# Modulation products of a two-block transformer moved from TensorE to GpSimd

## The chip, the cores and the metric

The kernel runs on one core of a Trainium2 chip. The time is that of the device for one execution, in microseconds (us). Three runs of the kernel before gave 2389.13, 2389.92 and 2393.08 us.

## The reference

Two depth layers (`i` = 0, 1) work on x (256 tokens of 1024 features), each with three sublayers: a SwiGLU feed-forward, an attention (forgetting attention in layer 0, dilated attention in layer 1), and a second SwiGLU. A second block without modulation follows. The part that is changed computes, for each layer, a vector of 9216 numbers from the single row c:

```
c_act = jax.nn.silu(c)
mod = (c_act @ mod_w[i] + mod_b[i]).reshape(B, 3, 3, D)
shift, scale, gate = mod[:, :, 0], mod[:, :, 1], mod[:, :, 2]
h = rms_norm(x, norm_g[i, s]) * (1 + scale[:, s]) + shift[:, s]
x = x + MACARON_WEIGHT * gate[:, s] * swiglu(h, ...)      # s = 0, 2; attention with gate alone for s = 1
```

All is float32. mod_w holds 2 x 1024 x 9216 numbers, 75 MB.

## The kernel before, in words

All weights pass through one stream of 411 pieces of mostly 1 MB (4 blocks of 128 rows by 512 columns), in the order in which TensorE (PE) uses them. SyncE issues their DMAs in that order into six buffers (`raw`, RAW = 6): the piece k goes where the piece k-6 lay, and its DMA waits until that one is free, with every later DMA behind it (L1251 to L1255). A weight piece ("w") is split by ScalarE (ACT) into `whi` and by VectorE (DVE) into the remainder `wlo` (three buffers of each, CONV = 3), which frees its raw buffer; PE then does three products of each block with the split activations. A modulation piece ("m") isn't split.

A modulation unit (i, u) is 512 of the 9216 columns, two m pieces (h = 0 and 1, with 4 blocks each). There are 36 units; the first four of layer 0 come before the first norm, the other 32 lie among the work of the sublayers. `mod_unit` lets PE do eight products in float32, the column of silu(c) (32 wide, one column filled) against 512 columns (L1352 to L1360), into four strips of one PSUM bank. ACT copies the bank to `mrow` (L1507), and after the next feature or token step PE turns `mrow` by four transposes (`mod_turn`, L1361), and DVE sums the four strips and adds the bias (L1682). The m piece's buffer is free when PE has done its products.

`stage_order` places the units. The norm of a sublayer has one, between the statistics and the rows (`between` in `norm`), but for the first norm. The first SwiGLU of layer 0 (stage A) has units 4 to 10 after gateup steps 0, 2, 4, 6, 9 and down steps 0 and 2. The forgetting attention (stage B) has unit 11 at its norm, then unit 12 after its first `fox_in` and `fox_f`, 13 and 14 after the second `fox_in`, 15 after the third. The other SwiGLUs with units (stages C, D and F) have one at the norm, one after gateup 0, and, but for F, four more after gateup 3, 6 and 9 and down 1. The dilated attention (stage E) has one at the norm and five behind groups of three projections. A gateup or token projection is two w pieces, a down step one. The shift and scale units must be done before the norm that reads them, the gate units before the sublayer's last update.

At the start of a sublayer is a `barrier`: ACT, DVE and GpSimd (POOL) wait for the last work planned so far on the others. POOL's program otherwise holds only small loads, the rope angles and, in the second block, the bias and decay tables.

Of the kernel before, what the change touches and what calls it, by code (L numbers as in the profile page):

```python
# [13 lines left out]
P = 128  # L14
# [6 lines left out]
CONV = 3  # L21
PIECE = 2048
BIG = 1e30
ALPHA = 4.0 ** 0.25
# [4 lines left out]
    "c_in", "mod_in", "ident_in", "x_in", "small_in", "late_in", "out_st",  # L29
    "const_set", "c_silu", "w_hi", "w_lo", "piece", "mod_mm", "mod_row", "mod_turned", "mod_col",  # L30
    "square", "stat", "diag", "sqrt", "recip", "rows", "scaled", "x_hi", "x_mod", "x_lo", "resid",
# [10 lines left out]
class Plan:  # L42
# [3 lines left out]
    def __init__(self, a):  # L46
        self.a = a
        self.steps = []
        self.count = {}
        self.recent = {}  # L50
        self.pieces = []
        self.next_dma = self.next_conv = self.use = self.n_conv = 0
        self.raw_free = [None] * RAW
        self.conv_free = [None] * CONV
        self.land = [0] * RAW
        self.free = [None] * 8
        self.pair = 0
        self.beside = []
        self.turns = []
        self.mod_turns = []  # L60
        self.mod_row_free = None
        self.mod_ready = {}
# [87 lines left out]

    def run_turns(self, mod_only=False):
        while self.turns and not mod_only:
            self.turns.pop(0)()
        while self.mod_turns:
            self.mod_turns.pop(0)()

# [55 lines left out]
    def mod_unit(self, i, u, bank, ahead=CONV):  # L212
        bank_free = self.free[bank]
        for h in range(2):
            pc = self.take(ahead)
            tok = self.ev("pe", "mod_mm")
            self.add("mod_mm", h=h, bank=bank, slot=pc["slot"], landed=pc["landed"], bank_free=bank_free if h == 0 else None)
            self.used(pc, tok)
        self.run_turns(True)
# [3 lines left out]
        self.mod_turns.append(lambda: self.mod_turn(i, u, bank, row))  # L223

    def mod_turn(self, i, u, bank, row):
        bank_free = self.free[bank]
        turned = self.ev("pe", "mod_turned")
        self.mod_row_free = turned
        col = self.ev("dve", "mod_col")
        s = self.add("mod_turn", i=i, u=u, bank=bank, bank_free=bank_free, mod_row=row, mod_turned=turned, mod_col=col,  # L230
                     shift_read=self.shift_read.get(u // 2))
        self.free[bank] = col
        tok = s["mod_bias"] = self.ev("dve", "mod_col")
        sub, kind = u // 6, (u % 6) // 2
        if u % 2:
            if kind:
                tok = self.ev("dve", "mod_col")
            self.mod_ready[(i, sub, kind)] = tok


# [12 lines left out]

    def rstd(self, stat, eps, src=G0, dst=G1, between=None):
# [7 lines left out]
        if between:  # L262
            between()
# [4 lines left out]
    def norm(self, i, s, buf, stat, between=None):  # L268
        rows = self.rstd(stat, 0, between=between)
        if (i, s) == (0, 0):  # L270
            self.ensure(1)
        self.pair = 0
        am, bm = self.mod_ready[(i, s, 0)], self.mod_ready[(i, s, 1)]
        pend = []
# [52 lines left out]
    def down(self, q, tail=None):  # L327
        bank_free = []
        if q == 0:
            self.run_turns()  # L330
# [258 lines left out]
class Program(Plan):  # L589
# [278 lines left out]
    def stage_order(self):  # L868
# [10 lines left out]
        def ffn(i, j):  # L879
# [9 lines left out]
            for q in range(11):  # L889
                step("down", i=i, j=j, q=q)  # L890
                if q < 5:
                    for m in at[11 + q]:
                        step("mod", i=m[0], u=m[1], bank=G3)

# [104 lines left out]
    def lay_out(self):  # L999
# [6 lines left out]
        for s in order:  # L1006
            k, i, u = s["kind"], s.get("i"), s.get("u")
            if k == "mod":
                if tail is None and u == 3:
# [3 lines left out]
                    tail.flush(0)  # L1013
                self.mod_unit(i, u, s.get("bank", D3) - u % 2, CONV if self.in_stage else 0)
            elif k == "norm":
# [8 lines left out]
                md = s["m"]  # L1024
                self.norm(i, s["s"], buf, tail.tok, (lambda: self.mod_unit(*md, D3 - md[1] % 2, 1)) if md else None)
                if s["s"] == 1:
# [7 lines left out]
            elif k == "down":  # L1034
                if s["q"] == FB // 2 - 1:
                    tail = Tail(self, self.update("gate", i, 2 * s["j"]), "split" if (i, s["j"]) == (1, 1) else "square")
                self.down(s["q"], tail)
# [8 lines left out]
            elif k == "dil_attn":  # L1046
                self.dil_attn(s["hh"])
            elif k == "mix_out":
                if u == 1:
                    tail = Tail(self, self.update("gate", i, 1), "square")  # L1050
                self.out_unit(u, "x", self.need_x, tail)
# [55 lines left out]
def build(nc, a, out):  # L1107
    root = ExitStack()
    with root:
# [152 lines left out]
        def pe_program():  # L1262
# [14 lines left out]
            for s in plan.steps:  # L1277
# [83 lines left out]
                elif k == "mod_turn":  # L1361
# [301 lines left out]
        def dve_program():  # L1663
# [5 lines left out]
            V.memset(epst[:, 0:1], 1e-6).then_inc(sem["const_set"])  # L1669
            V.memset(epst[:, 1:2], 1e-5).then_inc(sem["const_set"])  # L1670
            for s in plan.steps:
                k = s["kind"]
# [7 lines left out]
                elif k == "attn_begin":  # L1680
                    q.wait_ge(s["dve"])
                elif k == "mod_turn":  # L1682
                    i, u, sub, kind = s["i"], s["u"], s["u"] // 6, (s["u"] % 6) // 2
# [3 lines left out]
                    c0 = mod[:, 4 * u:4 * u + 4]  # L1687
                    V.tensor_reduce(c0, ps[:, s["bank"], :].rearrange("p (m g n) -> p m g n", m=4, g=4)[:, :, :, 0], AX.X,  # L1688
                                    ALU.add).then_inc(sem["mod_col"])
                    q.wait_ge(s["mod_col"])  # L1690
                    V.tensor_tensor(c0, c0, modb[:, i, 4 * u:4 * u + 4], ALU.add).then_inc(sem["mod_col"])
                    if u % 2 and kind:
# [246 lines left out]
        def pool_program():  # L1939
# [17 lines left out]
            for s in plan.steps:  # L1957
                k = s["kind"]
                if k == "barrier":
                    for t in s["toks"]:  # L1960
                        q.wait_ge(t)
                elif k == "rope_angles":
                    c1 = 6.28125
# [139 lines left out]
```

## Time and profile before

| | |
|---|---|
| profiled execution | 2388.34 us |
| its span, first to last instruction | 2387.0 us |
| mean granted PE clock | 0.990 |
| busy: PE, DVE, ACT, POOL | 2287.9, 1315.5, 1155.0, 59.8 us |
| median of three runs | 2389.92 us |

The span is nearly the whole of the execution's time, 1.3 us less. Busy time is the union of an engine's instructions. In rows of a timeline the first number is the start, the second the length, and x16 means sixteen instructions in a row merged into one line; a float32 product is two MATMUL records.

### The profile page before, as it was taken

What the parts mean: (1) busy time and instruction counts of PE and PEld (TensorE: products, weight loads), DVE (VectorE), ACT (ScalarE), POOL (GpSimd) and SP (SyncE); (2) the same over time, 40 slices, a digit from 0 to 9 for tenths busy, and PEclk for the clock granted to TensorE, in tenths of its full rate; (3) what the DMA queues carried; (4) which work ended last, traced back from release to release, by engine and by line L of the source; (5) the groups of instructions that cost most, each with busy time, mean ns of one, the idle gap of its engine ahead of it and who ended that gap; (6) DMA issues with size and microseconds to landing.
All of it is one profiled execution on the core that took longest, in us unless ns stands there. A gap on an engine that the chain in (4) does not pass through costs nothing.

```text
span 2387.0 us, 38790 instructions
## 1 busy us (share of the span) xinstructions
PE 2287.9 (96%) x17008; PEld 2093.1 (88%) x17008; DVE 1315.5 (55%) x1763; ACT 1155.0 (48%) x1348; POOL 59.8 (3%) x72
## 2 busy tenths in 40 slices
PE   6999998999999999899899999999999999999998
PEld 3999777999899978677799997899999988989998
DVE  2543554544554466456455445556786544666873
ACT  4443555543544354544454345654555446436553
POOL 2000000000000000000000011000000020000000
PEclk9999999999999999999999999999999999999999
DMA  8767562676576657246165555433655464445550
GB/s 308 263 232 266 204 228 66 212 247 242 165 263 210 237 184 257 98 159 212 36 213 188 184 196 170 157 127 124 212 177 195 134 215 129 154 142 174 180 195 18
DMA packets 273592, 439.78 MB, mean 184 GB/s; under 512 B 10656, under 2 KB 147152, under 8 KB 273296
## 3 DMA queue, kind: packets, MB, share of 16 engines
q1 hardware_dynamic: 270880, 429.07, 53.3%
q0 software_dynamic: 2256, 7.12, 0.9%
q8 instruction: 134, 2.20, 0.4%
q10 hardware_dynamic: 288, 1.11, 0.1%
q14 instruction: 34, 0.28, 0.0%
HBM read 436.22 MB, written 1.05 MB: 183 GB/s over the span
## 4 chain that ended last, share of the span: by engine, by line
PE 90%; ACT 4%; DVE 3%; DMA 1%; issue 1%; SPq 0%; POOL 0%; ACTq 0%; POOLq 0%; DVEq 0%
PE ps L1266 89%; DVE wlo L1675 1%; ACT whi L1488 1%; ACT PT L1488 1%; PE ps L1454 1%; PE ps L1366 1%; DMA raw<-in_mod_w 1%; ACT L1488 0%; ACT xhi L1488 0%; DMA raw<-in_fox_w_in 0%; ACT S L1488 0%; SPq L1255 0%; DVE x L1707 0%; DVE xlo L1753 0%; DMA raw<-in_ffn_w_down 0%
## 5 line engine op out<-in xcount | busy, mean ns | idle before, releaser
L1675 DVE TENSOR_TENSOR wlo<-raw,whi 128x2048 fp32r<-128x2048 f32 x339 | 769.0, 2274 | 592.3 <-ACT whi L1488 592.1
L1488 ACT ACTIVATE whi<-raw 128x2048 fp32r<-128x2048 f32 x339 | 640.8, 1895 | 424.1 <-PE ps L1266 388.2
L1266 PE MATMUL ps<-xhi,whi 128*128 128x256 f32 x2888 | 735.0, 286 | 14.1 <-ACT xhi L1488 11.3
L1266 PE MATMUL ps<-xhi,wlo 128*128 128x256 f32 x2888 | 729.3, 284 | 0.0
L1266 PEld LDWEIGHTS ps<-xhi,whi 128*128 128x128 f32 x2888 | 557.1, 193 | 28.2 <-issue 27.4
L1266 PEld LDWEIGHTS ps<-xhi,wlo 128*128 128x128 f32 x2888 | 557.1, 193 | 0.3
L1266 PE MATMUL ps<-xlo,whi 128*128 128x256 f32 x2888 | 472.0, 284 | 3.6 <-DVE xlo L1893 3.4
L1266 PEld LDWEIGHTS ps<-xlo,whi 128*128 128x128 f32 x2888 | 402.3, 193 | 4.4 <-DVE xlo L1893 3.8
L1266 PE MATMUL ps<-hhi,whi 128*128 128x256 f32 x1056 | 298.9, 283 | 0.9 <-DVE modc L1688 0.9
L1266 PE MATMUL ps<-hlo,whi 128*128 128x256 f32 x1056 | 298.4, 283 | 0.0
L1266 PE MATMUL ps<-hhi,wlo 128*128 128x256 f32 x1056 | 297.6, 282 | 0.0
L1266 PE MATMUL ps<-whi,xhi 128*128 128x512 f32 x608 | 242.5, 399 | 7.0 <-DVE wlo L1675 4.5
L1266 PE MATMUL ps<-wlo,xhi 128*128 128x512 f32 x608 | 238.3, 392 | 0.0
L1266 PEld LDWEIGHTS ps<-hhi,whi 128*128 128x128 f32 x1056 | 199.7, 189 | 5.1 <-issue 3.4
L1266 PEld LDWEIGHTS ps<-hhi,wlo 128*128 128x128 f32 x1056 | 198.9, 188 | 0.1
L1266 PEld LDWEIGHTS ps<-hlo,whi 128*128 128x128 f32 x1056 | 197.9, 187 | 0.0
L1266 PE MATMUL ps<-whi,xlo 128*128 128x512 f32 x608 | 188.7, 392 | 0.0
L1266 PEld LDWEIGHTS ps<-whi,xhi 128*128 128x128 f32 x608 | 115.0, 189 | 37.0 <-issue 8.3
L1266 PEld LDWEIGHTS ps<-whi,xlo 128*128 128x128 f32 x608 | 114.8, 189 | 24.8
L1266 PEld LDWEIGHTS ps<-wlo,xhi 128*128 128x128 f32 x608 | 115.1, 189 | 22.6
L1488 ACT ACTIVATE e<-ps 128x512 f32<-128x512 f32 (+1 forms) x48 | 30.4, 633 | 158.5 <-PE ps L1266 158.4
L1488 ACT ACTIVATE hhi<-e 128x512 fp32r<-128x512 f32 x66 | 41.7, 632 | 110.0 <-DVE e L1937 71.2
(220 smaller groups left out, 2043.3 us busy)
## 6 DMA issues: line engine op xcount, KB each, us to landing
raw<-in_mod_w SPq DMA_DIRECT2D x72, 1024.0 KB, 9.1
raw<-in_w_in SPq DMA_DIRECT2D x52, 1024.0 KB, 5.1
raw<-in_ffn_w_gate SPq DMA_DIRECT2D x88, 512.0 KB, 6.1
raw<-in_ffn_w_up SPq DMA_DIRECT2D x88, 512.0 KB, 7.5
raw<-in_ffn_w_down SPq DMA_DIRECT2D x44, 1024.0 KB, 6.6
raw<-in_w_up SPq DMA_DIRECT2D x88, 512.0 KB, 4.7
raw<-in_dil_w_in SPq DMA_DIRECT2D x36, 1024.0 KB, 6.4
raw<-in_w_down SPq DMA_DIRECT2D x22, 1024.0 KB, 4.9
```

Of the source, the lines that this page charges most:

```text
L1266: return nc.tensor.matmul(o, lhs, rhs, start=start, stop=stop, skip_group_check=True)
L1366: ins = nc.tensor.transpose(ps[:, s["bank"], m * P:(m + 1) * P], mrow[:, m * P:(m + 1) * P], ident[:, :])
L1454: ins = nc.tensor.transpose(ps[:, D0 + c // 2, (c % 2) * T + t * P:(c % 2) * T + (t + 1) * P], tms[s["name"]][:, t, c * P:(c + 1) * P], id ...
L1488: return nc.scalar.activation(o, i, func, **kw)
L1675: V.tensor_tensor(wlo[:, s["c"], 0:s["n"]], raw[:, s["slot"], 0:s["n"]], whi[:, s["c"], 0:s["n"]].bitcast(F32), ALU.subtract).then_inc(sem ...
```

## The change

The 32 units within the sublayers go another way; the first four stay as they are. Per half, POOL multiplies the four blocks in place in `raw` by silu(c), a scalar for each partition, adds two pairs in one instruction and then the two sums, and for h = 1 adds this to `mrow`. The m piece's buffer is free when POOL has done it. POOL may write `mrow` only after PE has read that of the unit before. PE then sums over the partitions: four float32 products of a 128 x 128 block of `mrow` with one column of ones (`mod_sum`), and DVE adds the bias from PSUM. ACT's copy, the transposes and the strips' reduction are gone for these units.

`mod_sum` of a unit comes in PE's order after the third feature, token or down step behind the unit's place, at the next unit's place if that comes sooner (`mod_beside` empties the list), or before its reader. The unit of a norm is now planned ahead of the norm.

```
@@ Plan
+    def run_mods(self, upto=None):
+        for m in self.mod_turns:
+            m[2] += 1
+        while self.mod_turns and (self.mod_turns[0][2] > MOD_LAG or upto and self.mod_turns[0][:2] <= list(upto)):
+            self.mod_turns.pop(0)[3]()
+    def mod_beside(self, i, u):
+        while self.mod_turns:
+            self.mod_turns.pop(0)[3]()
+        acc_free = self.mod_row_free
+        for h in range(2):
+            pc = self.take()
+            toks = [self.ev("mod", "mod_acc") for _ in range(3 + h)]
+            self.add("mod_acc", h=h, slot=pc["slot"], landed=pc["landed"], acc_free=acc_free, acc=toks)
+            self.used(pc, toks[-1])
+        self.mod_turns.append([i, u, 0, lambda: self.mod_sum(i, u, toks[-1])])
+    def mod_sum(self, i, u, acc):
+        bank = self.mod_bank
+        bank_free = self.free[bank]
+        summed = self.mod_row_free = self.ev("pe", "mod_turned")
...
@@ PE
+                elif k == "mod_sum":
+                    q.wait_ge(s["mod_acc"])
+                    q.wait_ge(s["bank_free"])
+                    q.wait_ge(("const_set", 5))
+                    for m in range(4):
+                        ins = mm(ps[:, s["bank"], m:m + 1], mrow[:, m * P:(m + 1) * P], epst[:, 2:3], m == 0, True)
+                    ins.then_inc(sem["mod_turned"])
@@ POOL
+                elif k == "mod_acc":
+                    q.wait_ge(("c_silu", 1))
+                    q.wait_ge(s["landed"])
+                    v = raw[:, s["slot"], :].rearrange("p (k n) -> p k n", k=4)
+                    for kk in range(4):
+                        ins = V.tensor_scalar(v[:, kk, :], v[:, kk, :], csil[:, 4 * s["h"] + kk, 0:1], None, ALU.mult)
+                    ins.then_inc(sem["mod_acc"])
+                    q.wait_ge(s["acc"][0])
+                    V.tensor_tensor(v[:, 0:2, :], v[:, 0:2, :], v[:, 2:4, :], ALU.add).then_inc(sem["mod_acc"])
+                    q.wait_ge(s["acc"][1])
+                    q.wait_ge(s["acc_free"])
+                    if s["h"] == 0:
+                        V.tensor_tensor(mrow[:, :], v[:, 0, :], v[:, 1, :], ALU.add).then_inc(sem["mod_acc"])
+                    else:
+                        V.tensor_tensor(v[:, 0, :], v[:, 0, :], v[:, 1, :], ALU.add).then_inc(sem["mod_acc"])
+                        q.wait_ge(s["acc"][2])
+                        V.tensor_tensor(mrow[:, :], mrow[:, :], v[:, 0, :], ALU.add).then_inc(sem["mod_acc"])
```

## Rows read from the trace of the kernel before

**Rows 1.** The page: the span, busy time by engine, and the chain that ended last.
```profile
span 2387.0 us, 38790 instructions
PE 2287.9 (96%) x17008; PEld 2093.1 (88%) x17008; DVE 1315.5 (55%) x1763; ACT 1155.0 (48%) x1348; POOL 59.8 (3%) x72
PE 90%; ACT 4%; DVE 3%; DMA 1%; issue 1%; SPq 0%; POOL 0%; ACTq 0%; POOLq 0%; DVEq 0%
```

**Rows 2.** The start and stage A: length, engines busy, granted clock, DMA share, GB/s.
```profile
0.00:36.50 36.50, 19.26 (x96) 6.54 (x96) 2.04 (x14) 8.15 (x16) 3.05 (x9) 1.00 0.99 349
36.50:261.30 224.80, 217.17 (x1760) 203.00 (x1760) 108.43 (x103) 97.06 (x95) 10.78 (x29) 0.98 0.68 232
```

**Rows 3.** PE's timeline, stage A: a unit's products, its transposes, and what follows each.
```profile
83.00 1.92 PE L1266 MATMUL ps<-raw,csil 128*32 128x512 f32 x16
84.85 0.39 PE L1266 MATMUL ps<-xhi,whi 128*128 128x256 f32 x1
...
96.46 0.60 PE L1366 MATMUL ps<-ident,mrow 128*128 128x128 f32 x4
96.82 0.36 PE L1266 MATMUL ps<-xhi,whi 128*128 128x256 f32 x1
...
110.35 0.39 PE L1266 MATMUL ps<-xhi,whi 128*128 128x256 f32 x1
...
193.17 0.39 PE L1266 MATMUL ps<-hhi,whi 128*128 128x256 f32 x1
```

**Rows 4.** Groups by line and form: count, busy us, mean ns, idle before.
```profile
L1266 PE MATMUL ps<-dg,S 128*128 128x128 f32 x512 | 74.6, 293 | 9.7 <-ACT PT L1488 7.9 <-DVE dg L1783 1.8
L1266 PEld LDWEIGHTS ps<-sqb,mean 128*128 128x128 f32 x160 | 29.1, 189 | 14.7 <-ACT sqb L1488 11.1
L1974 POOL TENSOR_SCALAR rp<-rp 128x32 f32<-128x32 f32 x2 | 0.6, 291 | 0.2
```

**Rows 5.** POOL's timeline: its large instructions, and the last before units 4 and 11.
```profile
47.36 0.21 POOL L1981 TENSOR_SCALAR rp<-rp 128x32 f32<-128x32 f32 x1
261.59 0.52 POOL L1950 DMA_DIRECT2D fbf<-in_fox_b_f  x1
1426.57 3.67 POOL L2005 TENSOR_SCALAR nbias<-nbias 128x1024 f32<-128x1024 f32 x1 [5.53 <-DMA nbias<-in_na_rpb]
1524.63 2.55 POOL L2010 TENSOR_TENSOR rd<-rd,rtm 128x512 f32<-128x512 f32 x2 [46.35 <-ACT rtm L1488]
1917.61 2.76 POOL L2005 TENSOR_SCALAR nbias<-nbias 128x1024 f32<-128x1024 f32 x1 [4.07 <-DMA nbias<-in_na_rpb]
```

**Rows 6.** DVE's timeline: the splits that overlap two of those instructions.
```profile
1425.31 2.29 DVE L1675 TENSOR_TENSOR wlo<-raw,whi 128x2048 fp32r<-128x2048 f32 x1 [4.42 <-ACT whi L1488]
...
1919.33 2.29 DVE L1675 TENSOR_TENSOR wlo<-raw,whi 128x2048 fp32r<-128x2048 f32 x1 [4.32 <-ACT whi L1488]
```

**Rows 7.** DMA issues by source: KB each, median us to landing.
```profile
raw<-in_w_in SPq DMA_DIRECT2D x52, 1024.0 KB, 5.1
```

**Rows 8.** Timelines of ACT and of DVE: one piece's split in stage A.
```profile
98.83 1.90 ACT L1488 ACTIVATE whi<-raw 128x2048 fp32r<-128x2048 f32 x1
...
100.77 2.29 DVE L1675 TENSOR_TENSOR wlo<-raw,whi 128x2048 fp32r<-128x2048 f32 x1 [1.11 <-ACT whi L1488]
```

**Rows 9.** PE's timeline, stage B: the norm's rows, unit 12, the fourth token step.
```profile
261.40 0.71 PE L1266 MATMUL ps<-ident,st 128*128 128x128 f32 x4
...
277.62 1.92 PE L1266 MATMUL ps<-raw,csil 128*32 128x512 f32 x16
...
313.58 0.50 PE L1266 MATMUL ps<-whi,xhi 128*128 128x512 f32 x1
```

**Rows 10.** DVE's timeline: the reciprocal on which those norm's rows wait.
```profile
260.98 0.17 DVE L1723 RECIPROCAL st<-st 128x2 f32<-128x2 f32 x1 [0.45 <-ACT st L1488]
```

**Rows 11.** PE's timeline, stage C: the norm's unit 16, and PE behind unit 17.
```profile
426.29 1.92 PE L1266 MATMUL ps<-raw,csil 128*32 128x512 f32 x16
...
444.06 0.39 PE L1266 MATMUL ps<-xhi,whi 128*128 128x256 f32 x1
```

More of the change, by code:

```diff
@@ L22 @@
 PIECE = 2048
+MOD_LAG = 2
 BIG = 1e30
@@ L29 @@
     "c_in", "mod_in", "ident_in", "x_in", "small_in", "late_in", "out_st",
-    "const_set", "c_silu", "w_hi", "w_lo", "piece", "mod_mm", "mod_row", "mod_turned", "mod_col",
+    "const_set", "c_silu", "w_hi", "w_lo", "piece", "mod_mm", "mod_row", "mod_turned", "mod_col", "mod_acc",
     "square", "stat", "diag", "sqrt", "recip", "rows", "scaled", "x_hi", "x_mod", "x_lo", "resid",
@@ L149, in used, with run_turns @@
         self.use += 1
-    def run_turns(self, mod_only=False):
-        while self.turns and not mod_only:
+    def run_turns(self):
+        while self.turns:
             self.turns.pop(0)()
-        while self.mod_turns:
-            self.mod_turns.pop(0)()
+        self.run_mods()
+    def run_mods(self, upto=None):
[3 more added lines that the diff above has]
+            self.mod_turns.pop(0)[3]()
     def run_beside(self):
@@ L222, in mod_unit @@
         self.free[bank] = row
-        self.mod_turns.append(lambda: self.mod_turn(i, u, bank, row))
+        self.mod_turns.append([i, u, MOD_LAG, lambda: self.mod_turn(i, u, bank, row)])
     def mod_turn(self, i, u, bank, row):
@@ L238, in mod_turn @@
             self.mod_ready[(i, sub, kind)] = tok
+    def mod_beside(self, i, u):
[12 more added lines that the diff above has]
+        summed = self.mod_row_free = self.ev("pe", "mod_turned")
+        s = self.add("mod_sum", i=i, u=u, bank=bank, bank_free=bank_free, mod_acc=acc, mod_turned=summed,
+                     shift_read=self.shift_read.get(u // 2))
+        self.mod_columns(s, i, u)
+        self.free[bank] = s["mod_bias"]
     def square(self, m, after):
@@ L252, in stat, with rstd @@
         return tok
-    def rstd(self, stat, eps, src=G0, dst=G1, between=None):
+    def rstd(self, stat, eps, src=G0, dst=G1):
         diag = self.ev("dve", "diag")
@@ L266, in rstd, with norm @@
         return rows
-    def norm(self, i, s, buf, stat, between=None):
-        rows = self.rstd(stat, 0, between=between)
+    def norm(self, i, s, buf, stat):
+        rows = self.rstd(stat, 0)
+        self.mod_bank = D2
         if (i, s) == (0, 0):
@@ L328, in down @@
         bank_free = []
+        self.mod_bank = G3
         if q == 0:
@@ L892, in ffn @@
                     for m in at[11 + q]:
-                        step("mod", i=m[0], u=m[1], bank=G3)
+                        step("mod", i=m[0], u=m[1])
         def mix(i):
@@ L1013, in lay_out @@
                     tail.flush(0)
-                self.mod_unit(i, u, s.get("bank", D3) - u % 2, CONV if self.in_stage else 0)
+                if self.in_stage:
+                    self.mod_beside(i, u)
+                else:
+                    self.mod_unit(i, u, D3 - u % 2, 0)
             elif k == "norm":
@@ L1024, in lay_out @@
                 md = s["m"]
-                self.norm(i, s["s"], buf, tail.tok, (lambda: self.mod_unit(*md, D3 - md[1] % 2, 1)) if md else None)
+                if md:
+                    self.mod_beside(*md)
+                self.norm(i, s["s"], buf, tail.tok)
                 if s["s"] == 1:
@@ L1681, in dve_program @@
                     q.wait_ge(s["dve"])
-                elif k == "mod_turn":
+                elif k in ("mod_turn", "mod_sum"):
                     i, u, sub, kind = s["i"], s["u"], s["u"] // 6, (s["u"] % 6) // 2
@@ L1687, in dve_program @@
                     c0 = mod[:, 4 * u:4 * u + 4]
[L1688 to L1691, printed above, removed]
+                    b0 = modb[:, i, 4 * u:4 * u + 4]
+                    if k == "mod_turn":
+                        V.tensor_reduce(c0, ps[:, s["bank"], :].rearrange("p (m g n) -> p m g n", m=4, g=4)[:, :, :, 0], AX.X,
+                                        ALU.add).then_inc(sem["mod_col"])
+                        q.wait_ge(s["mod_col"])
+                        V.tensor_tensor(c0, c0, b0, ALU.add).then_inc(sem["mod_col"])
+                    else:
+                        V.tensor_tensor(c0, ps[:, s["bank"], 0:4], b0, ALU.add).then_inc(sem["mod_col"])
                     if u % 2 and kind:
```

13 lines of the change are left out of this document (10 added, 3 removed).

## The prediction

> **What bounds the kernel now.** First the page: PE is busy 2287.9 of 2387.0 us and holds 90% of the chain that ended last [rows 1]; ACT and DVE are half free, POOL is nearly idle. Then the windows by stage: in stage A PE is busy 217 of 225 us while the DMAs are busy 0.68 of the time [rows 2]. So PE's own work is the bound, and the weight stream stays ahead of it only by a few pieces. Then the timelines around a unit, for what PE gives to the modulation and what stands behind a buffer.
>
> The stream's delay, from a free raw buffer to a piece that PE can use, I call D: landing 5.1 us in the median [rows 7], 4.6 us being the least that I take for a lone issue (an estimate from that row), then ACT's and DVE's split, 1.90 + 2.29 us, with hops 4.3 [rows 8]; together with 0.4 us until ACT starts 9.3 us. A second megabyte behind the first adds 1.05 MB at 349 GB/s [rows 2] = 3.0 us: 12.3 us.
>
> **Taken from PE.** The products delay the next step by 84.85 - 83.00 = 1.85 us, the transposes by 96.82 - 96.46 = 0.36 us [rows 3]. Of the 32 units five are a norm's. There the rows come at 261.40 and their reciprocal ends at 261.15 [rows 9, 10]: the products lie in a wait, and their going gives 0.2 us. So 27 x 1.85 + 32 x 0.36 = 61.5 us.
>
> **Added to PE.** Four float32 products are eight records. Each holds PE at most as long as a 128 x 128 one, 74.6 / 512 = 0.146 us, or a lone weight load of 0.189 us [rows 4]: 1.2 or 1.5 us. Below, four transposes with as many loads cost 0.36 us net [rows 3]. I take 0.8 us, since one column streams in less time than 128: 32 x 0.8 = 25.6 us. Net, were all else hidden: -36 us. ACT's copy (0.6 us) and DVE's reduction (0.2 us) lie beside PE; I count nothing for them.
>
> **POOL's time for a unit.** A scaling of 128 x 512 isn't in the trace. 128 x 1024 takes 2.76 us [rows 5] and 128 x 32 takes 0.29 us [rows 4]; the line between gives 1.49 us, half of the larger 1.38 us. A two-input add of 512 takes 2.55 / 2 = 1.27 us [rows 5]. I take 1.4, and 2.5 for an add of 1024. Half h = 0: 4 x 1.4 + 2.5 + 1.3 + 0.1 = 9.5 us; h = 1 has one add more, 10.9 us. A unit is 20.4 us undisturbed. Bounds: 19 us with scalings at the add's 1.27, 21.5 us with 1.49 and hops.
>
> It isn't undisturbed. The scaling that begins at 1426.57, within a split that ends at 1427.60, takes 3.67 instead of 2.76 us: it gets going only when the split is over. The split that begins within POOL's at 1919.33 keeps its 2.29 us, and POOL its 2.76 [rows 5, 6]. So each split stops POOL from the end of its current instruction (on average 0.8 us in) to the split's end: about 1.35 us lost per split. In stages A, C and D a split comes every 6 us or so, the factor is 6.2 / (6.2 - 1.35) = 1.28: h = 0 12.2, h = 1 14.0, the unit 26.2 us. In stage B PE waits much and splits are rare: 1.15, the unit 23.4 us; the same at the start of C. If POOL lost nothing it would be 20.4; if DVE's other two-input work stops it as well, I put 29 us in A.
>
> The Trainium skill (SBUF — State Buffer, Who interferes with whom) says that a VectorE instruction with two SBUF inputs and a GpSimd one that reads SBUF share an interface, that the one issued first has it whole, and the other blocks. The first pair of rows agrees; by the rule the splits would be late as well, behind POOL's instructions, which the second pair doesn't show. It would add up to some tenths of a us to D.
>
> **What POOL's time does to the path.** POOL holds a unit's two raw buffers until it has done each half; the DMA behind waits, and all behind that. POOL may write `mrow` for the next unit only after PE's `mod_sum`, which is late (third step, or next place). So from a place: sum 0.8, the last add of the half that waits 1.7, the second half 14.0, then D.
>
> Stage A. POOL begins unit 4 at 47.6, behind the rope angles [rows 5], and ends it at 73.8. The weight behind unit 5 is ready at 73.8 + 12.3 = 86.1; before, it started at 84.85 [rows 3]. With four w pieces (4 x 5.76 us) between places, the cycle is 0.8 + 1.7 + 14.0 + 12.3 = 28.8 us against 25.50 (110.35 - 84.85) before: the weight behind unit 6 comes at 112.2 (+1.9), behind unit 7 at 138.4 (+2.5). Six pieces to unit 8 hide it (+0.9). Down 1 is in the buffer of unit 8's second half: 173.0 + 0.8 + 1.7 + 14.0 + 9.4 = 198.9, before 193.17 [rows 3]: +5.7. From there POOL runs without a pause: unit 9 done at 215.7 where PE asks at 210.4 (+9), down 4 in its buffer (+11), unit 10 done at 241.9, asked for before down 6 at about 237 (+17). Stage A: +17 us.
>
> Stage B decides. POOL begins unit 11 at 262.1 [rows 5]. Units 13 and 14 are next to each other and 15 is one token step on; each next place makes PE wait for the unit before. So the fourth token step can't start before unit 14 is done: 262.1 + 4 x 23.4 + 0.2 + 0.8 = 356.7, before 313.58 [rows 9]: +43.1. The waits on the way (place 12, asked for at 277 [rows 9], done at 285.5; the step behind it, ready at 295; places 14 and 15) lie inside this. One more piece, in unit 14's second buffer: +2. Stage B: +45 us.
>
> Stages C and D. Unit 16 starts at the barrier, 426.3 [rows 11], done at 449.4; PE is there at 441.6. The step behind unit 17 starts at 450.4, before 444.06 [rows 11]: +6.3. The next w piece lies in unit 16's second buffer, 449.4 + 9.4 = 458.8: +2.6. The same behind unit 17: +3.2, and the weight behind the unit after it +2.2. Then three units at -1.5 each, hidden by six pieces, and one at four pieces, +3.4: about +12.8 us, in each of C and D. Stage E has six pieces between units and long attentions: -7 for PE's net saving, +4 for two late pieces at its start, -3 us. Stage F has only the norm's unit and the next: +6.3 + 2.6 + 3.2 - 0.4 = +11.7 us.
>
> Sum: 17 + 45 + 12.8 + 12.8 - 3 + 11.7 = 96 us. The profiled execution took 2388.34 us, 1.6 us under the median of the runs, which is within their spread: 2388.3 + 96 = 2484 us. What the 36 us saved on PE were to bring is in these terms.
>
> **Rivals.** (1) POOL loses nothing to DVE, a unit is 20.4 us. B is 262.1 + 81.6 + 1.0 - 313.6 + 2 = +33, A -6, C and D +3 each, E -7, F +7: +33, 2421 us. For it: one split and one POOL instruction overlap without loss [rows 5, 6]. Against it: the other pair. Chance 0.2. (2) It gets worse than I say: 29 us per unit in A, C, D, F and 26 in B. A +35, B +55, C and D +18 each, F +15, E -1: +140, 2528 us. For it: DVE has other two-input work, and late splits make D longer. 0.15. (3) The other side: the scaling reads one operand where the add reads two, so it may take half of the add's 1.27 us. Then a unit is 8 x 0.65 + 8.9 + 0.6 = 14.7 us. B is still 262.1 + 58.8 + 1.0 - 313.6 = +8, but A is -8, C and D -4 each, E -7, F +2: -13, 2375 us. It decides from about 17 us per unit, where the gains on PE and B's waits cancel (that case, no change, 0.02). Against it: 2.76 us for 1024 elements is even slower per element than the add [rows 5]. 0.07. The Trainium skill (GPSIMD Engine Reference, 4.1 Engine selection) has this rule: one-input work on GpSimd runs at about line rate, two-input work at half of VectorE's. The row says otherwise for the one-input half.
>
> **How the numbers follow.** Forecast 0.56, rivals 0.2, 0.15, 0.07, no change 0.02. 2484 us is the forecast's; its own range is 2455 to 2510. For 8 in 10 I go down to rival 1 and up nearly to rival 2: 2421 to 2526 us. Slower by over 0.2% (4.8 us, about what a measurement here can tell from no change): 0.91; within: 0.02; faster: 0.07.
>
> **What would show it.** In the profile after: POOL busy some 600 to 750 us, a scaling of 512 at 1.4 us undisturbed and longer under a split; PE's records fewer, its idle time up by over 100 us, named by POOL (`mrow`, before the sums) and by DVE's `wlo`; the longest wait before unit 13's sum, some 20 us, then unit 14's, about 10; 7 to 9 us before the sums of units 16, (1, 4) and (1, 16); stage B some 45 us longer than 166.7; PE's granted clock lower in places, behind long waits. The forecast is wrong if a scaling takes under 0.9 us, or if the buffers come free sooner than POOL's instructions say.

## The result, and the profile after

The kernel after takes 2600.55 us (median of 4 runs, 2596.61 to 2605.47), the kernel before on the same chip 2390.49 us: ratio 1.0878, 95% interval 1.0853 to 1.0903. The direction was right. The time lies 116 us above the forecast and 75 us above the end of the range: the forecast asked for 96 us of loss, 210 came.

The page of the kernel after, to be held against [rows 1]:
```profile
span 2595.3 us, 38385 instructions
PE 2299.9 (89%) x16624; PEld 2147.1 (83%) x16624; DVE 1395.9 (54%) x1732; ACT 1140.1 (44%) x1316; POOL 923.3 (36%) x488
PE 44%; DVE 2%; ACT 2%; POOL 0%; DMA 0%; issue 0%; SPq 0%; ACTq 0%; POOLq 0%; DVEq 0%
L1723 DVE TENSOR_TENSOR wlo<-raw,whi 128x2048 fp32r<-128x2048 f32 x339 | 818.5, 2421 | 786.4 <-ACT whi L1535 786.4
```
PE has 384 records fewer, yet is busy for 12 us more, and its share fell from 96% to 89%. POOL is busy for 923 us instead of 60, where 600 to 750 were forecast. The splits on DVE rose by 147 ns each (2274 ns before).

The windows by stage (length, then PE, PEld, DVE, ACT, POOL busy, PE's granted clock, DMA share, GB/s), from one norm's rows to the next: first B, C, E and F of the kernel before (A stands in [rows 2], D is as long as C), then A to F of the kernel after.
```profile
261.40:428.10 166.70, 155.83 (x980) 121.11 (x976) 92.60 (x213) 94.85 (x175) 0.71 (x2) 1.00 0.49 172
428.10:640.40 212.30, 209.52 (x1728) 198.88 (x1724) 102.91 (x96) 92.47 (x89) 0.00 (x0) 1.00 0.66 223
...
852.70:1206.10 353.40, 329.87 (x2065) 272.17 (x2061) 205.84 (x350) 176.02 (x226) 0.69 (x2) 0.98 0.44 157
1206.10:1659.00 452.90, 441.38 (x3281) 415.22 (x3277) 242.74 (x292) 215.19 (x222) 22.85 (x15) 0.99 0.55 179
```
```profile
37.80:316.00 278.20, 226.72 (x1661) 223.41 (x1661) 119.49 (x94) 93.40 (x88) 204.68 (x117) 0.87 0.54 186
316.00:553.10 237.10, 164.27 (x917) 133.53 (x917) 104.89 (x208) 94.50 (x170) 141.52 (x79) 0.82 0.36 125
553.10:802.80 249.70, 209.71 (x1652) 207.85 (x1652) 116.97 (x90) 89.61 (x83) 166.18 (x79) 0.91 0.55 190
802.80:1033.90 231.10, 209.13 (x1653) 206.85 (x1653) 117.09 (x90) 89.63 (x83) 150.24 (x71) 0.95 0.58 204
1033.90:1416.20 382.30, 326.47 (x1989) 276.35 (x1989) 233.39 (x344) 173.04 (x220) 185.78 (x90) 0.94 0.41 146
1416.20:1868.60 452.40, 440.87 (x3269) 416.58 (x3269) 242.37 (x289) 212.55 (x219) 49.29 (x29) 0.99 0.52 177
```
The stages lost 54.7, 70.4, 37.4, 18.8, 28.9 and -0.5 us. A wait ahead of a norm's rows ends the stage before that norm in these windows, though it belongs to the norm's unit. Put where it belongs (20.4 us each at the norms of C, D and F, 4.0 at E's: a wait of 22.15 or 5.74 us in the kernel after, less the 1.8 us that lay there before, filled by the unit's products), the losses are A 54.7, B 50.0, C 37.4, D 35.2, E 12.5, F 19.9, and -1.3 behind them: 208 us, the difference of the two spans.

In other terms: PE's idle time went from 92.5 to 288.8 us; its records other than the modulation's took 53 us longer (2199 us before, 2252 after); and the modulation's took 41 us less (88.5, now 47.3). That is 196 + 53 - 41 = 208 us. (All three are sums over PE's records, each counted up to the start of the next.)

### The profile page after: what moved, and what is told of

It is laid out like the page before. It is cut to its first block and busy times, and to the rows that moved or that the text cites. A ratio compares the mean times of both kernels' runs of the same rounds, so it can differ in the third digit from the quotient of the medians.

```text
span 2595.3 us, 38385 instructions
## 1 busy us (share of the span) xinstructions
PE 2299.9 (89%) x16624; PEld 2147.1 (83%) x16624; DVE 1395.9 (54%) x1732; ACT 1140.1 (44%) x1316; POOL 923.3 (36%) x488
## 5 line engine op out<-in xcount | busy, mean ns | idle before, releaser
L1723 DVE TENSOR_TENSOR wlo<-raw,whi 128x2048 fp32r<-128x2048 f32 x339 | 818.5, 2421 | 786.4 <-ACT whi L1535 786.4
L1306 PE MATMUL ps<-xhi,whi 128*128 128x256 f32 x2888 | 749.7, 290 | 58.5 <-DVE wlo L1723 47.2
L1306 PE MATMUL ps<-xhi,wlo 128*128 128x256 f32 x2888 | 743.2, 288 | 0.0
L2019 POOL TENSOR_SCALAR raw<-raw,csil 128x512 f32<-128x512 f32 x256 | 515.1, 2029 | 336.4 <-PE ps L1306 233.1
L1306 PEld LDWEIGHTS ps<-xhi,whi 128*128 128x128 f32 x2888 | 569.8, 197 | 63.0 <-issue 40.9
L1306 PEld LDWEIGHTS ps<-xhi,wlo 128*128 128x128 f32 x2888 | 569.5, 197 | 0.4
L1306 PE MATMUL ps<-xlo,whi 128*128 128x256 f32 x2888 | 478.8, 287 | 4.9 <-DVE xlo L1945 3.4
L1306 PEld LDWEIGHTS ps<-xlo,whi 128*128 128x128 f32 x2888 | 409.0, 196 | 5.9 <-DVE xlo L1945 3.8
L1306 PE MATMUL ps<-hhi,whi 128*128 128x256 f32 x1056 | 304.2, 288 | 11.3 <-DVE wlo L1723 11.3
L1306 PEld LDWEIGHTS ps<-hhi,whi 128*128 128x128 f32 x1056 | 206.5, 196 | 12.0 <-DVE wlo L1723 11.9
L2022 POOL TENSOR_TENSOR raw<-raw 128x1024 f32<-128x1024 f32 x64 | 168.8, 2638 | 5.3
```

The lines of the kernel that those rows point to most:

```text
L1306: return nc.tensor.matmul(o, lhs, rhs, start=start, stop=stop, skip_group_check=True)
L1723: V.tensor_tensor(wlo[:, s["c"], 0:s["n"]], raw[:, s["slot"], 0:s["n"]], whi[:, s["c"], 0:s["n"]].bitcast(F32), ALU.subtract).then_inc(sem ...
L2019: ins = V.tensor_scalar(v[:, kk, :], v[:, kk, :], csil[:, 4 * s["h"] + kk, 0:1], None, ALU.mult)
L2022: V.tensor_tensor(v[:, 0:2, :], v[:, 0:2, :], v[:, 2:4, :], ALU.add).then_inc(sem["mod_acc"])
```

## Where the time goes in the trace after

PE's waits in the kernel after (what it waited for: us, times, the longest):
```profile
PE ps L1306 <- DVE st L1775: 82.6, 10, 22.2
PE ps L1306 <- DVE wlo L1723: 69.2, 25, 5.2
PE ps L1306 <- POOL mrow L2030: 38.5, 6, 20.7
```
The forecast looked for the third and the second line. The first, the norm's reciprocals, is the longest, and was not in it. PE's timeline at four places (start, length, in brackets the idle time before and what ended it): two sums of stage B, the step behind them, and the rows of C's norm.
```profile
388.17 1.87 PE L1306 MATMUL ps<-epst,mrow 128*128 128x1 f32 x8 [20.66 <-POOL mrow L2030]
...
411.38 1.87 PE L1306 MATMUL ps<-epst,mrow 128*128 128x1 f32 x8 [7.01 <-POOL mrow L2030]
413.11 0.77 PE L1306 MATMUL ps<-whi,xhi 128*128 128x512 f32 x1
...
553.08 1.22 PE L1306 MATMUL ps<-ident,st 128*128 128x128 f32 x4 [22.15 <-DVE st L1775]
```
And ahead of those rows, the timelines of POOL, of ACT and of DVE:
```profile
531.03 6.18 POOL L2019 TENSOR_SCALAR raw<-raw,csil 128x512 f32<-128x512 f32 x4 [93.14 <-PE ps L1306]
537.30 2.34 POOL L2022 TENSOR_TENSOR raw<-raw 128x1024 f32<-128x1024 f32 x1
539.71 1.26 POOL L2026 TENSOR_TENSOR mrow<-raw 128x512 f32<-128x512 f32 x1
540.95 6.18 POOL L2019 TENSOR_SCALAR raw<-raw,csil 128x512 f32<-128x512 f32 x4
```
```profile
546.19 1.91 ACT L1535 ACTIVATE whi<-raw 128x2048 fp32r<-128x2048 f32 x1 [16.47 <-DMA raw<-in_ffn_w_up]
552.53 0.30 ACT L1535 ACTIVATE st<-st,epst 128x2 f32<-128x2 f32 x1 [4.43 <-DVE st L1773]
```
```profile
548.23 3.47 DVE L1723 TENSOR_TENSOR wlo<-raw,whi 128x2048 fp32r<-128x2048 f32 x1 [18.98 <-ACT whi L1535]
551.63 0.41 DVE L1770 TENSOR_TENSOR sqb<-ps,ident 128x256 f32<-128x256 f32 x1
...
552.86 0.17 DVE L1775 RECIPROCAL st<-st 128x2 f32<-128x2 f32 x1 [0.36 <-ACT st L1535]
```
These rows show a chain that begins with an order. `mod_beside` calls `take()` with its full look-ahead (3 pieces), and the change calls it ahead of `rstd`. So the split of the next weight stands ahead of the norm's root and reciprocal in ACT's and DVE's order. That weight lands only once POOL has done with a buffer (541 us; its DMA is issued at 541.4 and takes 4.6), and the norm, which needs nothing of it, waits behind it. In the kernel before the unit was planned between the statistics and the rows, with a look-ahead of 1.

In stage A, POOL's timeline shows a second order that nobody touched:
```profile
136.08 1.62 POOL L2030 TENSOR_TENSOR mrow<-mrow,raw 128x512 f32<-128x512 f32 x1
154.58 0.52 POOL L2053 TENSOR_TENSOR rope<-rp,inv 128x32 f32<-128x32 f32 x1 [16.87 <-ACT rp L1535]
155.08 9.46 POOL L2019 TENSOR_SCALAR raw<-raw,csil 128x512 f32<-128x512 f32 x4
```
The rope tables' multiplication waits for ACT's sines, which are planned at gate/up step 6. Before, POOL waited there with nothing behind it. Now unit 7 stands behind it.

## Experiments

**Does POOL lose time to DVE, and DVE to POOL?** Behind the last step of the kernel before I put groups of POOL's instructions as the change has them (four scalings of 512, an add of 1024, an add of 512), two groups alone and two beside each of three others.
```diff
+                for kk in range(4):
+                    ins = V.tensor_scalar(v[:, kk, :], v[:, kk, :], csil[:, kk, 0:1], None, ALU.mult)
+                step(ins)
+                step(V.tensor_tensor(v[:, 0:2, :], v[:, 0:2, :], v[:, 2:4, :], ALU.add))
+                step(V.tensor_tensor(v[:, 0, :], v[:, 0, :], v[:, 1, :], ALU.add))
...
+                    V.tensor_tensor(raw[:, 3, :], raw[:, 1, :], raw[:, 2, :], ALU.add).then_inc(sem["b_dve"])
+                else:
+                    V.tensor_tensor(raw[:, 3, 0:512], ps[:, D0, :], raw[:, 2, 0:512], ALU.add).then_inc(sem["b_dve"])
...
+                act(raw[:, 4, :], raw[:, 5, :], ACT.Copy).then_inc(sem["b_act"])
```


> The kernel before, with nothing of the change, and behind its last step a test of POOL's instructions in four phases of two groups each. A group is four scalings of 128x512 in place, one add of 128x1024, one of 128x512. Phase 1 alone; phase 2 beside DVE adding two SBUF operands of 128x2048 (12 times); phase 3 beside DVE adding a PSUM and an SBUF operand of 128x512; phase 4 beside ACT copying 128x2048 in SBUF. Theory (POOL and DVE's second SBUF operand exclude each other): four scalings 6.2 us in phases 1, 3 and 4, the adds 2.4 and 1.3 us; in phase 2 each of POOL's instructions waits for the end of a DVE add of 2.3 us, so a group takes 1.5 to 2.5 times its 10 us, and some of DVE's adds last up to 3.5 us. Rival (any traffic of DVE or ACT in SBUF slows POOL): phases 3 and 4 are slower as well, by a fifth or more.

POOL's timeline, a group alone, then one beside DVE's adds of two SBUF inputs, then one beside those with an input in PSUM; and DVE's timeline:
```profile
2386.88 6.19 POOL L2036 TENSOR_SCALAR raw<-raw,csil 128x512 f32<-128x512 f32 x4 [367.79 <-ACT x L1489]
2393.15 2.34 POOL L2038 TENSOR_TENSOR raw<-raw 128x1024 f32<-128x1024 f32 x1
2395.56 1.26 POOL L2039 TENSOR_TENSOR raw<-raw 128x512 f32<-128x512 f32 x1
...
2406.96 11.74 POOL L2036 TENSOR_SCALAR raw<-raw,csil 128x512 f32<-128x512 f32 x4
2418.79 3.38 POOL L2038 TENSOR_TENSOR raw<-raw 128x1024 f32<-128x1024 f32 x1
2422.25 3.19 POOL L2039 TENSOR_TENSOR raw<-raw 128x512 f32<-128x512 f32 x1
...
2443.93 6.18 POOL L2036 TENSOR_SCALAR raw<-raw,csil 128x512 f32<-128x512 f32 x4
```
```profile
2406.89 35.82 DVE L1949 TENSOR_TENSOR raw<-raw 128x2048 f32<-128x2048 f32 x12 [21.98 <-POOL raw L2039]
```
A scaling is 6.19 / 4 = 1.55 us, a group 10.0 us alone and 18.5 us (2406.96 to 2425.44) beside DVE. DVE's adds take 35.82 / 12 = 2.98 us with the hops between them (2.29 to 4.31 us each); 2.29 is what a split of that size takes alone [rows 8]. Beside a DVE instruction with an input in PSUM, and beside ACT, POOL loses nothing. So the theory held: both engines lose, POOL most. The Trainium skill (SBUF — State Buffer, Who interferes with whom) says that these two engines share an interface which one holds alone, so that the other waits. The run agrees that each loses by the other, with 18.5 against 10.0 us and 2.98 against 2.29. It doesn't agree that an instruction has the interface for its whole length: 12 x 2.29 = 27.5 us of adds and two groups of 9.8 us were done in 35.8 us, not in 47. My forecast counted POOL's part, and put DVE's at some tenths of a us per piece.

**Is it the norm's order?** The norm's unit put back between the statistics and the rows, with a look-ahead of 1 (so place and look-ahead change together; "the order" means both):
```diff
-                    self.mod_beside(*md)
-                self.norm(i, s["s"], buf, tail.tok)
+                    self.mod_flush()
+                self.norm(i, s["s"], buf, tail.tok, (lambda: self.mod_beside(*md, 1)) if md else None)
```


> The changed kernel, but the norm's unit is planned where the kernel before has it, between the statistics and the rows and looking one weight piece ahead, so that no weight split that waits for a POOL-held buffer stands in ACT's and DVE's order ahead of the norm's square root and reciprocal. Theory (three norms of 22.15 us idle PE, and one of 5.7, come from that order): these gaps go to under 1 us, but the next place then waits some 8 us for the unit, so that 9 to 14 us are gained at each of three and about 4 at the fourth: 2555 to 2572 us against 2600. Rival (POOL's time alone sets these starts, and the wait only moves): within 10 us of 2600. Other rival (the whole 22 us are the order's): 2530 us.

Measured: 2591.85 us, ratio 1.084 (1.082 to 1.086): 9 us of gain, so the rival held (within 10 us). The kernel's waits of PE, and its windows of C, D, E and F:
```profile
PE ps L1310 <- DVE wlo L1727: 76.5, 32, 6.0
PE ps L1310 <- POOL mrow L2034: 65.1, 10, 20.8
...
PE ps L1310 <- DVE st L1779: 16.1, 10, 2.2
```
```profile
534.10:777.50 243.40, 216.83 (x1653) 214.27 (x1653) 121.89 (x90) 89.49 (x83) 168.41 (x79) 0.92 0.57 195
777.50:1023.20 245.70, 214.13 (x1652) 211.41 (x1652) 115.07 (x90) 89.44 (x83) 173.37 (x81) 0.93 0.56 193
1023.20:1387.00 363.80, 327.34 (x1989) 275.87 (x1989) 231.00 (x344) 173.15 (x220) 165.25 (x80) 0.96 0.43 153
1387.00:1856.30 469.30, 446.02 (x3268) 421.25 (x3268) 249.33 (x290) 214.33 (x220) 70.23 (x41) 0.98 0.52 173
```
The wait at the reciprocals went from 82.6 to 16.1 us as expected. Half of these 66 us came back as waits for POOL's sums (38.5 to 65.1) and for splits (69.2 to 76.5), and PE's busy time rose by 16 us (2299.9 to 2316.1). With no long wait left at a norm, C, D, E and F still lose 31.1, 33.4, 10.4 and 16.4 us against the kernel before. The longest wait in the trace was not what bound: POOL's next unit would have been late anyway.

**How does the time follow POOL's time per unit?** Only two of the four blocks are scaled in each half (the modulation is then not computed):
```diff
-                    for kk in range(4):
+                    for kk in range(2):
                         ins = V.tensor_scalar(v[:, kk, :], ...)
```


> The changed kernel, leaving out half of the work in question: only two of the four blocks of each half are scaled by silu(c), so the modulation is another. All waits, pieces and orders stay. POOL's unit falls from 27.0 by 4 x 2.03 to about 19 us. Theory (stages A and B follow POOL's time per unit, B by four units' worth): B loses about 32 us, A about 30, each norm's wait 4, with less half-clock time behind the waits: 2490 to 2520 us against 2600. Rival (the waits come from where buffers and sums stand in the order, not from how long POOL takes): 2570 us or more.

Measured: 2478.76 us, ratio 1.0369 (1.0356 to 1.0383): the theory's side, and 11 us below its range. POOL's busy time per unit fell from 27.7 to 19.6 us in the median, the kernel's time by 122 us.

**Fewer units on POOL.** Eleven of the 32, the others as in the kernel before:
```diff
-                if self.in_stage:
+                if (i, u) in ON_POOL:
                     self.mod_beside(i, u)
```


> Eleven of the 32 units on POOL, those with six weight pieces or more to the next unit (three in stage C, three in D, five in E); the other 21, and each norm's, as in the kernel before. Theory (a unit that POOL does in the time of its neighbours is worth 1.85 + 0.36 - 0.94 = 1.27 us of PE): 11 x 1.27 = 14 us faster than before, 2376 us; C and D without the waits of the whole change. Rival (POOL's reads delay DVE's splits, and the buffers that it holds still make PE wait once per unit): 2385 to 2400 us.

Measured: 2403.45 us, ratio 1.0057 (1.0044 to 1.007), slower than the theory and the rival have it. Step by step most of POOL's units brought 1.1 to 1.9 us, but 7.1 and 4.4 us went in the down steps behind units (1, 2) and (1, 8), where the next unit follows after four weight pieces, and 1 us at each norm, from my edit (a transposition came due just at the rows). Stage B, which has no unit on POOL here, was 5.7 us longer as well (172.4 us), with PE busy for 5.7 us more and its granted clock at 0.96 instead of 1.00. So a part of the loss is the clock's, and not POOL's.

**The wait for the sines**, taken away by order (`rope_mul` is POOL's multiplication, now behind unit 10):
```diff
+                if (i, s["j"]) == (0, 0) and s["q"] == 3:
+                    self.rope_mul()
```


> The kernel after, with GpSimd's one multiplication of the rotation tables (it waits for ScalarE's sines) moved in GpSimd's order from ahead of the modulation's unit 7 to behind its unit 10; ScalarE's sines stay where they are. In the kernel after, GpSimd stood 16.9 us in that wait in the first SwiGLU, between units 6 and 7, with a piece of modulation weights landed behind it. Theory (my forecast for this stage missed that wait): the weights behind unit 7 come 12 to 17 us earlier, the stage's loss falls from 54.7 us to 38 to 43, and the kernel takes 2584 to 2589 us. Rival (the units behind it are late by their own length, and take the gap back): the stage's loss stays within 4 us of 54.7, and the kernel takes 2597 to 2602 us.

Measured: 2588.43 us, ratio 1.0822 (1.0808 to 1.0837). Stage A's loss fell from 54.7 to 39.0 us, and B's stayed at 70.4. The theory held: 12 us of the time, 15.7 in the profiled stage. POOL's timeline in place of the gap:
```profile
140.16 1.29 POOL L2036 TENSOR_TENSOR mrow<-mrow,raw 128x512 f32<-128x512 f32 x1
141.44 6.19 POOL L2025 TENSOR_SCALAR raw<-raw,csil 128x512 f32<-128x512 f32 x4
```

**Does the slow clock behind a wait cost anything?** The granted clock of PE is 0.87 in A and 0.82 in B (0.98 and 1.00 before), since behind nearly each wait PE runs a stretch at 1.2 GHz. Dummy products were put into waits, ahead of four sums and three norms' rows; the lines for the rows:
```diff
+                    for _ in range(WARM_ROWS.get(nrows[0], 0)):
+                        mm(ps[:, s["bank"], 256:384], mean[:, :], mean[:, :], True, True)
                     q.wait_ge(s["recip"])
```


> The kernel after, with float32 128x128 products whose sum is thrown away put into TensorE's waits for seven of the longest stalls (ahead of the sums of units 8, 11, 13 and 14 of layer 0, 28, 12, 64 and 24 of them, and ahead of the rows of the third, fourth and sixth norm, 68 each), sized below the waits there. No work of the kernel is changed. In the kernel after, a stretch at half clock stands behind nearly each wait, and the steps' durations hold 52 us more than at the full clock beyond before's 26. Theory (that excess is a cost of its own, beside the waits): the half-clock stretches behind these seven waits go, each 1.3 to 2.6 us or more, and the kernel takes 2580 to 2592 us with a mean granted clock over 0.95. Rival (work in the shadow of a wait that GpSimd sets costs nothing, the next wait takes it back): 2597 to 2603 us, with the higher clock all the same.

Measured: 2616.97 us, ratio 1.094 (1.0926 to 1.0955), slower than either theory. The kernel's group of dummies shows why: PE waited first for their bank, 11.3 and 13.3 us, so the products began when the wait was all but over, and stood in the path. A and B, where the four sums lie, are 8.1 and 5.4 us longer than in the kernel after.
```profile
L1308 PE MATMUL ps<-mean 128*128 128x128 f32 x664 | 79.8, 284 | 24.6 <-DVE modc L1751 13.3 <-DVE e L1817 11.3
```
At the norms they filled 15.4 of 22 us, and the clock fell in the rest. This run tells nothing of the clock, so it was made again with the norms alone, sized to the wait:
```diff
-WARM = {(0, 8): 28, (0, 11): 12, (0, 13): 64, (0, 14): 24}
-WARM_ROWS = {3: 68, 4: 68, 6: 68}
+WARM = {}
+WARM_ROWS = {3: 98, 4: 98, 6: 98}
```


> The kernel after, with 98 float32 128x128 products (sum thrown away) ahead of the rows of the third, fourth and sixth norm alone: they took 0.226 us each in the last run of this kind, so 22.1 us, the whole wait there. In that run 68 left the last 7 us of each wait empty, and the clock fell all the same. Theory (the slow clock behind a wait costs the path): rows and the first weight take 0.7 and 5.9 us instead of 1.2 and 7.2 to 7.7, and each of the three stages is about 2 us shorter: 2594 us. Rival (the step behind them waits for a weight or for GpSimd's sum and takes it back): the first steps are shorter, the stages are not: 2599 to 2602 us.

Measured: 2597.23 us, ratio 1.0861 (1.0843 to 1.0879), between theory and rival, its interval over that of the kernel after. So the stages have to tell. PE at C's norm and behind D's, and the window of C:
```profile
558.23 0.71 PE L1308 MATMUL ps<-ident,st 128*128 128x128 f32 x4 [0.30 <-DVE st L1783]
...
809.82 0.41 PE L1308 MATMUL ps<-xhi,wlo 128*128 128x256 f32 x1
```
```profile
558.20:807.70 249.50, 229.60 (x1849) 227.75 (x1849) 112.51 (x90) 89.50 (x83) 170.19 (x80) 0.97 0.55 190
```
At C's norm the wait is filled (0.30 us left), the rows take 0.71 instead of 1.22 us, the first weight 6.0 instead of 7.5. Yet C is 249.5 us long, where it was 249.7. What the clock gave, later waits took: the rival held, at this one place. At D's and F's norms the rows took 0.71 us too, but the clock fell within the first weight all the same (products of 0.41 us instead of 0.28), so these two test nothing. Whether the slow stretches in A and B cost anything stays open; where PE waits for nobody they do, as stage B of the kernel with eleven units shows.

**What is left when POOL's work is gone?** The same instructions in the same order, all but one add of a unit (the first into `mrow`) cut to 8 columns per block, so that the modulation is not computed:
```diff
-  V.tensor_scalar(v[:, kk, :], v[:, kk, :], csil[:, 4 * s["h"] + kk, 0:1], None, ALU.mult)
+  V.tensor_scalar(v[:, kk, 0:8], v[:, kk, 0:8], csil[:, 4 * s["h"] + kk, 0:1], None, ALU.mult)
```


> The kernel after, with GpSimd's instructions of the units kept in number, order and waits, but cut to 8 columns of each block (all but the first addition of each unit): most of the modulation's scaling and adding is left out. It gives the change's floor. Theory (all that the change costs is the time of GpSimd's instructions; order, waits and the column sums cost nothing): 2350 to 2362 us, the time before less the 36 us of TensorE's products and transposes that my forecast took off, and no wait of TensorE for a sum over 1 us. Rival (the order by which GpSimd holds the weight buffers, its wait for the sines, and the split planned ahead of each norm cost on their own): 2370 to 2400 us.

Measured: 2408.48 us, ratio 1.0073 (1.0058 to 1.0089): the rival's side, 8 us above its range. Even with units of 7.1 us the change costs time. ACT at C's norm shows the same chain as in the kernel after, and PE's waits name it:
```profile
430.63 1.91 ACT L1535 ACTIVATE whi<-raw 128x2048 fp32r<-128x2048 f32 x1 [9.77 <-DMA raw<-in_ffn_w_up]
435.78 0.29 ACT L1535 ACTIVATE st<-st,epst 128x2 f32<-128x2 f32 x1 [3.24 <-DVE st L1773]
```
```profile
PE ps L1306 <- DVE st L1775: 59.1, 10, 14.4
```

**The order again, where POOL's work no longer covers it**, on the floor kernel and on the one with half the scalings; the edit is that of the second experiment.

> The floor kernel (GpSimd's instructions cut to 8 columns, so most of the modulation's scaling and adding is left out) with the norm's unit planned between the statistics and the row factors, as in the kernel before. The floor kernel took 2408 us, where TensorE's saved products alone would give 2359 (27 units in the stages at 1.14 us each): in it TensorE starts the row factors 12.5 us late at three norms and 4.0 us at a fourth, though GpSimd's units take only 7 us. Theory (the split of the next weights, planned ahead of the norm's statistics by two pieces more than before, is a cost of the order alone): those waits go, and with the 2 us behind each the kernel takes 2355 to 2368 us. Rival (the wait only moves to the next sum or weight, as it did in the kernel with GpSimd's full work, which gained 9 us by this edit): 2396 to 2408 us.

> The same move of the norm's unit on the kernel in which GpSimd scales two of the four blocks of each half (the modulation is not computed; that kernel took 2479 us). Theory (the two causes compete: how much the order costs depends on whether GpSimd's units would set the same starts anyway, so that the edit's worth falls from some 45 us at units of 7 us to 9 us at units of 28 us): with units of 20 us in between, 2445 to 2465 us. Rival (anything near full work hides it): 2469 to 2479 us.

Measured: 2361.87 us (ratio 0.9881, 0.9858 to 0.9904) and 2443.80 us (1.0221, 1.0203 to 1.0239). PE's wait for the reciprocals in the first:
```profile
PE ps L1310 <- DVE st L1779: 16.1, 10, 2.2
```
With the runs above that makes a table, in us:

| POOL busy per unit (median) | order of the change | norm's order put back | the order's cost |
|---|---|---|---|
| 7.1 | 2408.5 | 2361.9 | 46.6 |
| 19.6 to 19.9 | 2478.8 | 2443.8 | 35.0 |
| 27.7 to 28.4 | 2600.6 | 2591.9 | 8.7 |

The first theory held; the second has its direction and misses its range by 1 us. (The 2359 us in the first expectation count 1.14 us per unit, while this floor kernel's trace has 1.59, as shown below. With it they are 2349, so some 13 us of cost stay with the order put back; what they are is open.) The same edit is worth 47 us or 9, by what else sets the starts. And with the order put back, POOL's time alone costs 82 us on its first 12.8 us (6.4 per us of a unit), then 148 us on the next 8.5 (17 per us).

**A version that gains.** Nine units, each with three weight units or more to the next modulation unit, and the transposition's place mended:
```diff
+ON_POOL = {(0, 10), (1, 0), (1, 1), (1, 6), (1, 7), (1, 11), (1, 12), (1, 14), (1, 17)}
...
-            m[2] += 1
+            m[2] += not upto
```


> Nine of the 32 units go to GpSimd (unit 10 of layer 0; units 0, 1, 6, 7, 11, 12, 14 and 17 of layer 1), each where three weight units or more follow before the next modulation unit, in stages in which TensorE waits for no weight; the other units are TensorE's as in the kernel before. Eleven units gave 2403 us, with a gain of 1.1 to 1.9 us for most of them, and losses of 4 to 7 us at two units close ahead of another one (1,2 and 1,8) and of 1 us at each norm from the place of a transposition; both are mended here. Theory (the change is worth TensorE's 1.1 to 1.9 us where GpSimd's unit has time to spare): 2376 to 2386 us, faster than both kernels. Rival (VectorE's splits beside GpSimd's additions and held buffers eat it everywhere): 2388 to 2398 us.

Measured: 2383.72 us (6 runs), ratio 0.9968 (0.9957 to 0.998): the theory held, 7 us or 0.3% under the kernel before. C and D are 209.1 and 209.0 us long, 3.2 and 3.3 less than before; in E, where three of the nine lie, 2.7 us are lost, and B, where none lies, lost 1.9.

## Why the prediction was wrong

**Right.** What bounds the kernel, the direction, and the mechanism: buffers held by POOL, weights late. PE's net term: in the floor kernel PE goes from the step behind one unit of stage A to that behind the next in 107.46 - 83.55 = 23.91 us, before in 25.50 [rows 3]; that is 1.59 us per unit (the 1.14 in an expectation above left out the transposes), where the forecast had 1.85 + 0.36 - 0.8 = 1.41. The undisturbed half: 9.9 us for 9.5, with a scaling at 1.55 for 1.4. Stage B: the token step behind unit 14 starts at 413.11 instead of 313.58 us [rows 9]: 99.5 us later, of which 54.6 came in from A: 44.9, forecast 43.1. It isn't luck: POOL's four units there take 95.0 us (316.3 to 411.3), forecast 93.6. The waits for sums 13 and 14 are 20.66 and 7.01, forecast about 20 and 10. Of the 7 to 9 us forecast before the sum of unit 16 nothing shows in the kernel after, where the norm's wait covers it; with the order put back they are 6.88.

**Wrong, the norms.** "There the products lie in a wait, and their going gives 0.2 us" priced the move of the norm's unit as pure PE work. The diff moves the call ahead of `rstd`, with a longer look-ahead, and by that the next weight's split ahead of the root and the reciprocal. It was to be read in the diff. It shows as 20.4 us at each of three norms and 4.0 at a fourth: 65 us, nearly all by which C, D, E and F lie above the forecast in this trace (105.0 us against 34.3). But taken away alone it gives 9 us. So 9 us are the order's alone, and most of the rest of these waits has two causes, either of which is enough: the order, or POOL's long units at the norm.

**Wrong, the terms of C, D and F.** With the order put back C to F still lose 91.3 us, 57 more than the forecast. For C the forecast's terms make +14.3 us behind unit 18 (6.3 + 2.6 + 3.2 + 2.2), then "three units at -1.5 each, hidden by six pieces", and +3.4 for the one at four pieces. In that run the steps behind units 18 and 20 start at 605.76 and 684.3 us, before at 481.09 and 555.13; less the 106.0 us by which the stage began later, they are late by 18.7 and by 23.2 us. So two units that were to give back 3 us cost 4.5, and the rest of the stage 8 more. Units 17 to 21 span 28.7 to 32.7 us there, not 26.2. POOL also waits 8.5 to 9.7 us for the DMA of the modulation's own weights ahead of units 18, 19 and 20, since they come through the same stream; the forecast let a unit start at its place. No run parts these two.

**Wrong, the wait for the sines.** I read POOL's idle time before as room. 16.9 us of it was a wait in POOL's order that a unit now stands behind. Taking it away gave 12 us (15.7 in stage A, where 37.7 us were missing in the forecast's 17).

**Wrong in size, POOL's factor and what follows from it.** I took 26.2 us per unit in A, C and D. The seven units of A span 26.9 to 30.9 us, 29.1 in the mean. The scalings of the kernel after:
```profile
L2019 POOL TENSOR_SCALAR raw<-raw,csil 128x512 f32<-128x512 f32 x256 | 515.1, 2029 | 336.4 <-PE ps L1306 233.1 <-DMA raw<-in_mod_w 103.1
```
A scaling takes 2029 ns in the mean, 31% over its 1.55; I had put 28% in these stages, and on 1.4. The first unit shows it: it takes from 47.6 to 78.2 us, 30.6, and the weight behind unit 5 starts at 91.7 us, forecast 86.1. Seven units by 2.9 us are 20 us: with the sines' 15.7 that would make 36 of stage A's missing 37.7, a count that no run shows by itself. The forecast's conversion was too flat as well: from 20.4 to 26.2 us per unit it went up by 63 us (rival 1 to forecast), 11 per us. The table has 17 in that range. That slope contains DVE's own loss (147 ns on each of 339 splits) and the slower clock; I have no run that parts them.

**The rivals.** Rival 2 (29 us per unit) had the unit's length and 2528 us, still 72 short of the measured time: the two orders and the flat conversion were missing there too. Rival 1 (POOL loses nothing) fell with the first experiment. Rival 3 (a scaling at half the add's time) fell with the 1.55 us. In the range I took in the unknown of one number and left out that a step could be missing.

## What to carry to other kernels

When work moves to an idle engine, look at its whole order for waits that were harmless while nothing stood behind them, and at everything a moved call plans (look-ahead, splits, DMA issues), not at its own instructions alone. An edit's worth depends on which other wait is due at the same moment: the norm's order was worth 47 us, 35 or 9. Before trusting the longest line of a list of waits, ask what would be late next. And here the idle engine was worth giving work only at the places where its whole time fits ahead of the next unit: nine units brought 7 us, 32 cost 210.

## What the runs showed of the hardware

- POOL's scaling with one full SBUF input is slower than its two-input add: 1.55 against 1.26 us for 512 elements per partition. The Trainium skill (GPSIMD Engine Reference, 4.1 Engine selection) has one-input work at about line rate and two-input work at half of VectorE's speed; the add agrees (2.34 us for 1024 columns, where DVE takes 2.29 for 2048), and for the scaling the measurement says otherwise.
- The cost of the clash is mutual: continuous two-input work from SBUF on both engines took POOL from 10.0 to 18.5 us per group and DVE from 2.29 to 2.98 us per 2048. It is not whole exclusion: 47 us of work were done in 35.8. A DVE input in PSUM, or ACT's work, cost POOL nothing.
- A scaling of 8 columns still takes 0.44 us on POOL, so 13 small instructions per unit are 7 us with one full add among them.
- A PE that was kept busy through a 22 us wait kept its full clock at C's norm (rows 0.71 us instead of 1.22, and the first weight too), and the kernel gained nothing, since another engine set a later start. At F's norm, filled just as far (0.30 us left), the clock fell within the first weight.
- The lower clock does cost where PE waits for nobody: stage B of the kernel with eleven units on POOL has none of them, and took 172.4 us at a granted clock of 0.96, 166.7 at 1.00.
